# The last expert's rows are added to x on TensorE and VectorE instead of through DRAM, and the router product runs in four column groups

## The reference, cut to what matters

```python
def grouped_moe(h, w_router, router_bias, w_gate, w_up, w_down):
    x = h.reshape(B * T, D)
    s = jax.nn.sigmoid((x @ w_router).astype(F32))
    ...                                   # the best group, then the best 2 experts in it
    a = jnp.einsum('nd,edf->nef', x, w_gate)
    u = jnp.einsum('nd,edf->nef', x, w_up)
    act = jax.nn.silu(a) * u * gate[..., None].astype(x.dtype)
    return jnp.einsum('nef,efd->nd', act, w_down).reshape(B, T, D)

for i in range(DEPTH):
    ...                                   # x = x + g1 * mixer(norm(x))
    xs = xs + g2s * grouped_moe(rmsnorm(xs, norm2[i]) * (1.0 + sc2s) + sh2s, ...)
y_sample = rmsnorm(xs, norm_final)
```

## Time and profile before

| | us |
|---|---|
| median of 3 runs | 1872.56 (1870.21 to 1872.79) |
| the profiled execution | 1873.76 |
| its span, first to last instruction | 1871.8 |
| TensorE busy | 1706.0 (91%) |
| VectorE, ScalarE, POOL busy | 628.8, 249.8, 187.8 |
| mean granted TensorE clock | 0.954 of full |

### The profile page before, as it was taken

How to read it: one execution, slowest core, us unless ns; L and a number is a source line. 1 busy time by engine, 2 the same in 40 slices (tenths; PEclk the granted TensorE clock), 3 DMA queues, 4 the chain that set the end, 5 groups by cost and what they waited for, 6 DMA issues and landing times.

```text
span 1871.8 us, 16701 instructions
## 1 busy us (share of the span) xinstructions
PE 1706.0 (91%) x6142; PEld 960.9 (51%) x6142; DVE 628.8 (34%) x1090; ACT 249.8 (13%) x528; POOL 187.8 (10%) x276
## 2 busy tenths in 40 slices
PE   4999989999999999999978999598999999789993
PEld 2864375644764456644454444254666665544441
DVE  2333323343233342333452332222333324423322
ACT  5000000000000000000111111221323221111111
POOL 1000000010001100010001222110000000012222
PEclk8999999999999999999978999798999999789996
DMA  9423452124312251212673999830000033749995
GB/s 340 156 90 135 160 205 81 46 90 139 142 45 90 90 190 45 90 48 87 191 280 114 345 345 330 254 108 0 23 21 6 7 83 120 243 127 344 345 332 146
DMA packets 159646, 282.26 MB, mean 151 GB/s; under 512 B 11460, under 2 KB 106456, under 8 KB 154472
## 3 DMA queue, kind: packets, MB, share of 16 engines
q1 hardware_dynamic: 144616, 236.39, 36.2%
q0 software_dynamic: 9536, 34.66, 7.2%
q10 hardware_dynamic: 5440, 10.49, 1.6%
HBM read 247.09 MB, written 34.42 MB: 150 GB/s over the span
## 4 chain that ended last, share of the span: by engine, by line
PE 78%; DMA 7%; SPq 7%; DVE 3%; issue 2%; ACT 1%; ACTq 0%; POOL 0%; DVEq 0%; POOLq 0%
PE banks L1110 15%; PE banks L1000 10%; PE banks L975 8%; PE banks L1171 7%; PE banks L1279 4%; PE banks L1378 4%; PE banks L1188 3%; SPq L595 3%; PE banks L1102 3%; PE banks L1094 3%; SPq L596 3%; PE banks L1085 2%; PE banks L885 2%; DMA wr<-in_moe_w_down 2%; PE banks L1310 2%
## 5 line engine op out<-in xcount | busy, mean ns | idle before, releaser
L1110 PE MATMUL banks<-wr 128*128 128x512 f32 x640 | 281.3, 592 | 0.0
L1171 PE MATMUL banks<-wr,arena 128*128 128x512 f32 x512 | 232.2, 607 | 9.7 <-DMA wr<-in_moe_w_down 6.6
L1110 PEld LDWEIGHTS banks<-wr 128*128 128x128 f32 x640 | 119.4, 190 | 139.7 <-issue 139.7
L1000 PE MATMUL banks<-wr 128*128 128x256 f32 x768 | 173.3, 385 | 4.0 <-ACT arena L1485 2.4
L1000 PEld LDWEIGHTS banks<-wr 128*128 128x128 f32 x768 | 147.8, 193 | 29.2 <-issue 4.5
L1171 PEld LDWEIGHTS banks<-wr,arena 128*128 128x128 f32 x512 | 96.9, 194 | 124.1 <-issue 123.1
L975 PE MATMUL banks<-wr,arena 128*128 128x512 f32 x320 | 142.5, 600 | 2.4 <-ACT arena L1479 2.4
L1188 PE MATMUL banks<-wr,arena 128*128 128x512 f32 x256 | 115.4, 593 | 0.9 <-ACT arena L1569 0.9
L975 PEld LDWEIGHTS banks<-wr,arena 128*128 128x128 f32 x320 | 60.3, 193 | 73.0 <-issue 71.5
L1519 ACT ACTIVATE arena<-banks 128x512 f32<-128x512 f32 x40 | 23.9, 597 | 520.4 <-PE banks L1110 520.4
L809 POOL DMA_INDIRECT acc_dram<-arena,put_ids x32 | 64.2, 2005 | 274.3 <-DVE arena L2023 263.3
(11 more groups left out here) (261 smaller groups left out, 1956.5 us busy)
## 6 DMA issues: line engine op xcount, KB each, us to landing
wr<-in_w_ada SPq DMA_DIRECT2D x24, 2048.0 KB, 7.6
wr<-in_moe_w_gate SPq DMA_DIRECT2D x32, 1024.0 KB, 12.9
wr<-in_moe_w_up SPq DMA_DIRECT2D x32, 1024.0 KB, 15.6
wr<-in_moe_w_down SPq DMA_DIRECT2D x32, 1024.0 KB, 15.7
wr<-in_ret_w_in SPq DMA_DIRECT2D x12, 2048.0 KB, 10.7
wr<-in_ret_w_in SPq DMA_DIRECT2D x8, 1024.0 KB, 8.7
wr<-in_ret_w_out SPq DMA_DIRECT2D x4, 2048.0 KB, 7.7
arena<-mod_rows_dram SPq DMA_DIRECT2D x14, 512.0 KB, 7.3
```

The lines of the kernel that those rows point to most:

```text
L1000: mm = mmul(dst[:, r * 256:r * 256 + 256], lhs, rhs, start=(start and r == 0 and k == 0), stop=(k == 3), skip_group_check=True)
L1110: mm = mmul(bank[i % 3][:], hT[:, k, tile_cols(t)], ring8(2 + r)[:, k, :], start=(k == 0), stop=(k == KT - 1))
L1171: mm = mmul(bank[2][:], xgT[:, e.par, k, :], expert_w(e.buf)[0][:, k].rearrange("p g f -> p (g f)"), start=(k == 0), stop=(k == KT - 1))
```

## The change

Two parts, and a clearing up of semaphores.

*The last expert.* POOL no longer runs `put(15)`; SP's `x_back` waits for the other 15 scatters. VectorE builds, after the third expert, a matrix `last_tok` of zeros and ones (rows are expert 15's slots, columns the 640 tokens). After the last down product TensorE multiplies it with expert 15's scaled rows (`ysb[:, 1]`), two products of 512 columns per tile, into banks 4/5, 6/7, 2/3, 4/5, 6/7; VectorE adds each tile's product to the x that was loaded. The square of tile t waits for that add instead of the load. `last_tok` and `ysb` lie where layer 1 keeps other things, so `latent(0)` and SP's loads of the cached keys and what follows them wait for these products or adds.

*The router.* The router's weights become the stationary operand, 32 columns at a time (16 wanted, 16 that are ignored), the transposed tokens stream with 128 columns, and four column groups of the array each take two of the eight blocks of the contraction. ScalarE copies the [4 x 32, 128] result (`router_copy`), and one more product with a 0/1 matrix (`router_sum`, `pick16`) adds the four groups and turns the tile back to tokens by experts.

```diff
@@ TensorE
+                if t:
+                    router_sum(l, t - 1)
+                elif l == 0:
+                    pe.wait_ge(S("ada_act"), 10)
+                for i in range(2):
+                    for g in range(4):
+                        k = 2 * g + i
+                        mm = mmul(bank[ST_BANK[l]][32 * g:32 * g + 32, 0:P], w_rt[:, NE * k:NE * k + 32], h2T[:, t % 2, k, :],
+                                  start=(i == 0), stop=(i == 1), tile_position=(0, 32 * g))
                 mm.then_inc(S("router_mm"), 1)
+            def router_sum(l, t):
+                pe.wait_ge(S("rt_copied"), l * NT + t + 1)
+                mmul(bank[R_BANK[l]][:, t * NE:(t + 1) * NE], s_T[:, tile_cols(t)], pick16[:], start=True, stop=True)\
+                    .then_inc(S("rt_sum"), 1)
...
                 overflow(pe, l)
+                pe.wait_ge(S("yd"), l * NE + NE)
+                pe.wait_ge(S("pick2_set"), l + 4)
+                for t in range(NT):
+                    if t >= 3:
+                        pe.wait_ge(S("x_add"), 10 * RH + l * NT + t - 2)
+                    b0 = (4, 6, 2, 4, 6)[t]
+                    for hf in range(2):
+                        mm = mmul(bank[b0 + hf][:], last_tok[:, tile_cols(t)], ysb[:, 1, hf * 512:hf * 512 + 512],
+                                  start=True, stop=True)
+                    mm.then_inc(S("op_done"), 1)
@@ ScalarE
-                    act.wait_ge(S(f"x_back{t}"), 16 + 16 * (n // 2))
+                    act.wait_ge(S("x_add"), 10 * RH + (n // 2 - 1) * NT + t + 1)
+            def router_copy(l, t):
+                act.wait_ge(S("router_mm"), l * NT + t + 1)
+                A_(s_T[:, tile_cols(t)], bank[ST_BANK[l]][:, 0:P], ACT.Copy).then_inc(S("rt_copied"), 1)
...
+                router_copy(l, NT - 2)
                 h2_evac(l, NT - 1)
-                act.wait_ge(S("router_mm"), l * NT + NT)
+                router_copy(l, NT - 1)
+                act.wait_ge(S("rt_sum"), l * NT + NT)
@@ VectorE
+                for t in range(NT):
+                    ins = v.tensor_scalar(last_tok[:, tile_cols(t)], row_no[:], float(t * P + 1), got_ids[:, NE - 1:NE],
+                                          ALU.add, ALU.is_equal)
...
                 overflow(dve, l)
+                for t in range(NT):
+                    dve.wait_ge(S(f"x_back{t}"), 32 + 16 * l)
+                    dve.wait_ge(S("op_done"), 10 * RH + l * NT + t + 1)
+                    v.tensor_tensor(x[:, t, :], x[:, t, :], banks((4, 6, 2, 4, 6)[t], 2), ALU.add).then_inc(S("x_add"), 1)
@@ POOL and SP
-                put(NE - 1)
-                sp.wait_ge(S("y_out1"), l * 128 + 128)
+                sp.wait_ge(S("y_out1"), l * 112 + 112)
+            sp.wait_ge(S("op_done"), 10 * RH + NT)
             sp.dma_start(c_kpe[:, 0:64], a["cache_mla_kpe"][0, 0]).then_inc(S("tab_in"), 16)
@@ semaphores that now share a counter
-            act.wait_ge(S("lg_in"), 16)
+            act.wait_ge(S("vec_in"), 112)
-            pe.wait_ge(S("vec_in"), 96)
+            pe.wait_ge(S("vec_in"), 112)
```

More of the change, by code:

```diff
@@ L70 @@
 R_BANK = (2, 6)
+ST_BANK = (3, 7)
 def use_base(h):
@@ L179, in build @@
         stage = sb("stage", [P, 512])
-        pick2 = sb("pick2", [P, 2])
-        w_rt = sb("w_rt", [P, KT, NE])
+        pick16 = sb("pick16", [P, NE])
+        pick2 = pick16[:, 0:2]
+        w_rt = sb("w_rt", [P, KT * NE + NE])
         bias_row = sb("bias_row", [P, NE])
@@ L297, in build @@
         rt = [M["rt"][:, 80 * i:80 * i + 80].rearrange("p (t e) -> p t e", t=NT) for i in range(12)]
+        last_tok = M["h2"][:, 0:T]
+        s_T = M["rt"][:, 0:T]
         rq = [M["rt"][:, 960 + 20 * i:980 + 20 * i] for i in range(12)]
@@ L505, in overflow @@
                     eng.wait_ge(S(f"ov_out{l}"), 16 * NE * nb)
+                if who == "pe":
+                    eng.wait_ge(S(f"ov_ev{l}"), 4 * NE * nb)
         @block.sync
@@ L806, in put @@
                     else:
-                        pool.wait_ge(S(f"y_out{1 - b}"), l * 128 + 16 * ((e + 1) // 2))
+                        pool.wait_ge(S(f"y_out{1 - b}"), l * (128 if b else 112) + 16 * ((e + 1) // 2))
                     alone(pool)
@@ L900, in chunk_sum @@
                 for m in range(4):
-                    mm = mmul(bank[j % 4][:, 2 * m:2 * m + 2], stage[:, tile_cols(m)], pick2[:], start=True, stop=True)
+                    mm = mmul(bank[j % 4][:, 2 * m:2 * m + 2], stage[:, tile_cols(m)], pick2, start=True, stop=True)
                 mm.then_inc(S("proj_done"), 1)
@@ L930, in router @@
                 pe.wait_ge(S("hTd"), n * NT + t + 1)
-                for k in range(KT):
-                    mm = mmul(bank[R_BANK[l]][:, t * NE:(t + 1) * NE], h2T[:, t % 2, k, :], w_rt[:, k, :],
-                              start=(k == 0), stop=(k == KT - 1))
+                if t:
[7 more added lines that the diff above has]
+                                  start=(i == 0), stop=(i == 1), tile_position=(0, 32 * g))
                 mm.then_inc(S("router_mm"), 1)
+            def router_sum(l, t):
+                pe.wait_ge(S("rt_copied"), l * NT + t + 1)
+                mmul(bank[R_BANK[l]][:, t * NE:(t + 1) * NE], s_T[:, tile_cols(t)], pick16[:], start=True, stop=True)\
+                    .then_inc(S("rt_sum"), 1)
             pe.wait_ge(S("set_a"), 19)
-            pe.wait_ge(S("pick2_set"), 2)
+            pe.wait_ge(S("pick2_set"), 3)
             for j, (kind, c) in enumerate(PRE_ORDER):
@@ L1140, in moe @@
                 router(l, NT - 1)
+                router_sum(l, NT - 1)
                 pe.wait_ge(S("sel"), l + 1)
@@ L1237, in latent @@
                     pe.wait_ge(S("mw_in"), 32)
+                    pe.wait_ge(S("x_add"), 10 * RH + NT)
                 if t >= 2:
@@ L1531, in rows_evac @@
             def rows_evac(l):
-                act.wait_ge(S("rows_T"), l + 1)
+                act.wait_ge(S("rows_T"), l + 2)
                 if l:
                     act.wait_ge(S("rows_out0"), 16)
-                A_(mod_rows[:], bank[4][0:96, 0:P], ACT.Copy).then_inc(S("rows_sb"), 1)
+                A_(mod_rows[:], bank[4][0:96, 0:P], ACT.Copy).then_inc(S("set_a"), 1)
             head(0)
@@ L1547, in _ @@
                     h2_evac(0, t - 1)
+                if t >= 2:
+                    router_copy(0, t - 2)
                 if t + 2 < NT:
@@ L1683, in _ @@
                     h2_evac(1, t - 1)
+                if t >= 2:
+                    router_copy(1, t - 2)
                 if t + 2 < NT:
@@ L1756, in _ @@
             v.memset(cond[:, 16:46], 0.0).then_inc(S("pick2_set"), 1)
-            v.tensor_reduce(pick2[:], ident[:].rearrange("p (g c) -> p c g", g=4)[:, 0:2, :], AX.X, ALU.add)\
+            v.memset(w_rt[:, KT * NE:KT * NE + NE], 0.0).then_inc(S("pick2_set"), 1)
+            v.tensor_reduce(pick16[:], ident[:].rearrange("p (g c) -> p c g", g=4)[:, 0:NE, :], AX.X, ALU.add)\
                 .then_inc(S("pick2_set"), 1)
@@ L1894, in _ @@
             x_sums()
-            dve.wait_ge(S("mask_tri"), 2)
+            dve.wait_ge(S("gset"), 23)
             dve.wait_ge(S("set_a"), 2)
@@ L2021, in y_evac @@
                     if not (isinstance(e.n, int) and e.n < 2):
-                        dve.wait_ge(S(f"y_out{e.par}"), l * 128 + e.half * 16)
+                        dve.wait_ge(S(f"y_out{e.par}"), l * (112 if e.par else 128) + e.half * 16)
                     v.tensor_tensor(ysb[:, e.par, :], banks(4 + 2 * e.par, 2), gate2, ALU.mult).then_inc(S("yd"), 1)
@@ L2036, in moe @@
                     one(fixed(u, 4))
+                dve.wait_ge(S("h2_first"), 16 * l + 16)
+                dve.wait_ge(S("h2_out"), (16 * NT - 16) * (l + 1))
+                for t in range(NT):
+                    ins = v.tensor_scalar(last_tok[:, tile_cols(t)], row_no[:], float(t * P + 1), got_ids[:, NE - 1:NE],
+                                          ALU.add, ALU.is_equal)
+                ins.then_inc(S("pick2_set"), 1)
                 with dve.Fori(0, 3) as i:
```

18 lines of the change are left out of this document (9 added, 9 removed).

## The result

| | median us | ratio, 95% interval |
|---|---|---|
| before | 1872.67 | |
| the changed kernel | 1862.38 (1860.02 to 1863.88) | 0.9941 (0.9927 to 0.9955) |
| forecast | 1863.1 (1858.5 to 1868.5) | 0.9949 |

What follows compares the result with a forecast made beforehand. TensorE held 78% of the chain; uncovered were two DRAM scatters and the load of x ending each expert layer. Gains 5.2 + 1.2 + 2 x 1.55 = 9.5 us off 1872.56 gave 1863.1 us, range 1858.5 to 1868.5.

Steps and rivals of the forecast that it cites:

- The early load of x: End of both expert layers: without expert 15's scatter, the load of x goes out 6.8 and 6.9 us earlier.
- The fall of the clock in the pause: End of layer 0: TensorE idles 3.8 us before tile 3, and its clock falls to half.
- the late tiles: TensorE's products for tiles 3 and 4, behind the pause: 5.2 us, between 3.44 at full and 6.88 at half clock.
- rival 1: Clock stays up in the new pauses or comes back at once: 13.2 us gained, 1859.4 us; chance 0.15.
- the tail: End of layer 0, to the first attention product: gain 5.2 us, bounds 2.1 and 7.4.
- Layer 1's tail: End of layer 1: first final norm sooner, then stores and norms as before; gain 1.2 us, bounds -0.4 and 2.7.
- The router: Router blocks of tiles 0 and 1 shorten, 0.95 us a block: gain 1.55 us per layer, bounds -0.25 and 2.55.
- the last block: Last router block, 3.56 us, becomes sum, product, copy and the now uncovered 1.28 us table load: 3.6 us, no gain.
- At nothing: Side work such as building the 0/1 matrix and SP's delayed loads costs nothing; the matrix, if uncovered, 1.2 us a layer.
- Rival 2: Late products stay at half clock and issue sets the router: 1.2 us gained, 1871.4 us; chance 0.12.
- Rival 3: Router column groups do not overlap, each weight load waits for the product before: slower, 1895 us; chance 0.03.
- Rival 4: The early x does not reach the attention layer, something else being late: 4.3 us gained, 1868.3 us; chance 0.05.

Runs made afterwards that it cites:

- e3: The changed kernel plus unread TensorE products (four in layer 0, three in layer 1) filling the pause before tile 3; 0.9937 of the kernel before, median 1858.92 us.
- e9: e3 plus two more unread products in layer 0's next pause, between the transposes of tiles 0 and 1; 0.9922 of the kernel before.
- e1: The changed kernel with the router of before, so only the last-expert part is kept; 0.9965 of the kernel before, 6.6 us less.
- e5: The changed kernel with a tile's eight router products one behind the other in one column group instead of four; run once, 1859.3 us.
- e6: The changed kernel with a small sigmoid on ScalarE ahead of the last router copy, so its table loads earlier; 0.9922 of the kernel before.
- e2: The changed kernel with the last expert scattered to DRAM as before, so only the router part is kept; 0.9981 of the kernel before, 3.6 us less.
- e7: The changed kernel with the first final norm ahead of the adds of tiles 3 and 4 and a buffer per final tile; 0.9936, median 1860.49 us.
- e8: The changed kernel with the edits of e4, e6 and e7 together; 0.9913 of the kernel before, 1856.0 us.
- e10: e9 with the edits of e6 and e7 added; 0.9914 of the kernel before.
- e11: e10 with the last two tiles' scales taken off GpSimd, onto ScalarE and VectorE; 1850.04 us, 0.9877 of the kernel before.
- e0: The changed kernel run once more, unaltered; 0.9948 of the kernel before.
- e4: The changed kernel with other banks, so four tiles are multiplied before x arrives and only tile 4 waits; 0.9938 of the kernel before.

## Why the prediction was right, point by point

**The early load of x.** Forecast 5.5 and 5.0 us behind the start of expert 15's scaling; it was 5.53 and 4.88. From its issue to the first add 3.46 and 3.52, forecast 3.47 and 3.6. Right to a tenth, since each term was a row of before at the same place.

**The fall of the clock in the pause, the late tiles, the attention layer.** Pause forecast 3.8, measured 3.57 and 2.97. The clock fell, as forecast against rival 1. The term that missed is the late tiles': I took the middle of the two clocks, 5.2, and layer 0 took 6.33, nearly the half-clock end (6.88). So the first attention product came 20.3 us behind the scaling and not 19.4. But the clock was back by then, and that product took 7.03 us instead of the 7.76 of the earlier trace rows: the 0.7 us which I had put into the upper bound alone. Two misses of 0.9 and 0.7 cancel, and the tail gave 4.9 to 5.1 us (5.2 forecast). e3 and e9 show that the mechanism is the clock, and that it has to be followed further than the late tiles: full clock for them alone is worth 0.2 to 0.4 us, not 2.9, because the clock then falls at the next pause and takes 1.7 of the 1.9 us that reach the attention layer.

**Layer 1's tail** was sized too small: 1.2 forecast, 2.6 measured, at the edge of its bounds (2.7). The first norm came 16.0 us behind the scaling, 16.4 forecast, 17.7 before: 1.7 of gain. The step that failed is "from there on stores and norms alternate as before", as far as it meant that the end follows the first norm as before. The end moved 0.9 further, because before the change GpSimd's drain outlasted the last store by 0.9 us, and its last small operations now come sooner. I had followed the chain of waits to the last norm and had taken what lies behind it as fixed. Where the clock did not fall in that pause, in e1, e5 and e6, the same code gave 3.8 to 4.0: rival 1, in that layer. What decides between the two is not known.

**The router.** 1.55 forecast, 2.30 measured in both layers, within the bounds (2.55). A block takes 0.64 (0.57 to the next start) where I took 0.95; it came nearer to the floor of 0.46 than to the ceiling, and no run shows a price of the mode change that I had allowed for. Blocks of tiles 0 and 1 gave 1.13 and 0.91 instead of 0.9 and 0.65. The rest is the last block: from the sum of tile 3 to the sigmoid 3.25 us instead of the 3.60 before, where I saw no gain. That the table load would stand behind the copy uncovered was right (it does, 963.41), but TensorE's last sum runs beside half of it: e6 prices the uncovered half at 0.6 us a layer.

**At nothing.** The 0/1 matrix and SP's delayed loads: the expert stages move by -0.4 to +0.6 in the two profiles of the changed kernel, with both signs, and in e2, which has neither, by 0.0. The other kernels with the 0/1 matrix lie between -1.5 and +0.7, so a loss below a microsecond could not be told.

**The sum.** 5.2 + 1.2 + 3.1 = 9.5 forecast. By the ledger 5.0 + 2.6 + 4.6 = 12.2, and the two profiles that have the same code lose 0.3 to 0.5 in the attention stage and 0.3 to 0.6 among the experts of layer 1. The medians say 10.3. The sum came out close because two terms were too small (tail 1 by 1.4, the router by 1.5), while the stages in between gave some of it back and the profile of before lay 1.2 above its median. The total was right partly by such cancelling, and that is luck. e1 and e2 (6.6 and 3.6 against 6.4 and 3.1) agree with the parts, but within intervals too wide to show misses of this size; the stages show them.

**Rivals.** Rival 2 had the late tiles of layer 0 (6.3) and nothing else. Rival 3 falls with e5. Rival 4 falls with the first attention product, 4.3 us sooner behind expert 15's scaling than before (7.4 in the span). "DMA: Bandwidth & Descriptors" of the Trainium skill would have made the removed scatters worth 5.7 us less in all; e1 measured 6.6 us for what the rows made 6.4, so the rows were the better price.

## What to carry to other kernels

Price a removed transfer by its own row at that place, and then ask what else has been waiting there: the two scatters gone were worth 12 us by their rows and 7.6 at the end. A late product behind a pause costs its length at half clock, but before it is sped up, the step behind it has to be looked at; filling one pause moved the fall of the clock to the next, and only both together paid. And the end of a program belongs to the engine that stops last, not to the last store: let the slow one finish its small work early.

## What had not been expected of the hardware

- GpSimd's drain takes 6.0 to 7.1 us from its last small operation on and ends 5.4 to 5.6 us behind the end of that operation, in all fourteen profiles; in the kernel before and in e7, e8 and e10 it ended the execution.
- GpSimd's operations on 128x1 take 0.19 and 0.55 us. The 32 of them in these profiles that began while a final norm of VectorE was under way (0.05 us or more behind its start) took 0.8 to 1.6; the six that began ahead of the norm or together with it kept their length, so the order of the starts decides. It was so in the kernel before already:

```profile
1857.64 0.57 POOL L747 TENSOR_TENSOR rs<-rs,half 128x1 f32<-128x1 f32 x1
...
1860.36 1.28 POOL L746 TENSOR_SCALAR rs<-ss 128x1 f32<-128x1 f32 x1
...
1862.63 1.60 POOL L747 TENSOR_TENSOR rs<-rs,half 128x1 f32<-128x1 f32 x1
```

  Beside an add, which reads x and a bank, they keep their length even when they begin behind it (in e11, 0.55 at 1838.22). "SBUF — State Buffer" of the Trainium skill (Who interferes with whom) says that a VectorE instruction with two inputs in SBUF contends with a GpSimd instruction that reads SBUF, and one with a single such input, outside the modes that use two ports, does not. The rows agree in both cases.
- Equal code meets the clock differently. Late in the attention stage, where TensorE waits for VectorE several times in a row, the clock fell in the changed kernel, in e0, e1, e3, e4, e6, e7 and e11, and cost 1.4 to 1.7 us there; before the change, and in e2, e5, e8, e9 and e10, it did not. Nearer the start of that stage the clock differs too and moves it by up to 1.7 us, so the sum of the column alone does not tell the two kinds apart. The stretches in the changed kernel (columns as above):

```profile
1522.00:1524.00 2.00, 1.06 (x5) 1.09 (x6) 0.69 (x1) 0.60 (x1) 0.00 (x0) 0.67 0.99 294
1524.00:1526.00 2.00, 2.00 (x7) 1.35 (x6) 0.69 (x1) 0.60 (x1) 0.00 (x0) 0.50 0.86 251
```

  From 1517 on TensorE waited for VectorE four times, 0.5 to 0.9 us each; the clock fell in the fourth. What decides between the two outcomes was not tried and stays open.
